# Block inverse of the second recurrence: transposes by VectorE on 32 by 32 blocks in place of TensorE

## The reference

```python
def wkv_scan(r, v, decay, k, a_in, b_in, s0, reverse):
    def step(S, inp):
        rt, vt, wt, kt, at, bt = inp
        sa = jnp.einsum('bhij,bhj->bhi', S, at)
        S = S * wt[:, :, None, :] + sa[..., None] * bt[:, :, None, :] + vt[..., None] * kt[:, :, None, :]
        return S, jnp.einsum('bhij,bhj->bhi', S, rt)
    xs = tuple(jnp.moveaxis(z, 1, 0) for z in (r, v, decay, k, a_in, b_in))
    s_end, ys = lax.scan(step, s0, xs, reverse=reverse)
    return jnp.moveaxis(ys, 0, 1), s_end
```

## Time and profile before

| | |
|---|---|
| median of three runs | 3336.87 us |
| the profiled execution, its own time | 3332.58 us |
| its span, first to last instruction | 3330.8 us |
| PE (TensorE matmul) busy | 3237.4 us, 97% of the span |
| PEld (TensorE weight load) busy | 2940.8 us, 88% |
| DVE (VectorE) busy | 2141.8 us, 64% |
| ACT (ScalarE) busy | 1547.5 us, 46% |
| mean granted TensorE clock | 0.992 of full speed |
| the 16 batches of the recurrence | about 2395 to 3150 us from the span's start |

### The profile page before, as it was taken

How to read it: one execution, slowest core, us unless ns; L and a number is a source line. 1 busy time by engine, 2 the same in 40 slices (tenths; PEclk the granted TensorE clock), 3 DMA queues, 4 the chain that set the end, 5 groups by cost and what they waited for, 6 DMA issues and landing times.

```text
span 3330.8 us, 82761 instructions
## 1 busy us (share of the span) xinstructions
PE 3237.4 (97%) x37068; PEld 2940.8 (88%) x37068; DVE 2141.8 (64%) x3294; ACT 1547.5 (46%) x2366; POOL 177.1 (5%) x254
## 2 busy tenths in 40 slices
PE   7999999999899999999999999999999999999988
PEld 7989999899788888888889888988889999999987
DVE  7655755667668888885555544445666766657565
ACT  5433443445444444444434444433555555556433
POOL 0000000000000000000001010001211101111010
PEclk9999999999999999999999999999999999999999
DMA  5645655765455555555553343435443344434464
GB/s 202 237 165 176 210 209 188 286 252 198 143 176 189 191 190 190 189 191 203 187 188 125 119 148 123 152 122 171 159 137 129 121 143 130 144 126 135 132 231 152
DMA packets 99713, 571.20 MB, mean 171 GB/s; under 512 B 19856, under 2 KB 26288, under 8 KB 37408
## 3 DMA queue, kind: packets, MB, share of 16 engines
q1 hardware_dynamic: 85872, 511.85, 44.5%
q0 software_dynamic: 13488, 54.06, 4.8%
HBM read 535.59 MB, written 30.28 MB: 170 GB/s over the span
## 4 chain that ended last, share of the span: by engine, by line
PE 85%; DVE 7%; issue 3%; ACT 3%; DMA 1%; POOL 0%; DVEq 0%; SPq 0%; ACTq 0%; POOLq 0%
PE banks L300 15%; PE banks L301 8%; PE banks L1069 4%; PE banks L2209 4%; PE banks L1070 4%; PE banks L1071 4%; PE banks L324 3%; PE banks L325 3%; PE banks L326 3%; PE banks L2210 3%; PE banks L2211 3%; PE banks L2431 3%; PE banks L287 3%; PE banks L288 3%; PE banks L289 3%
## 5 line engine op out<-in xcount | busy, mean ns | idle before, releaser
L267 DVE TENSOR_TENSOR w_lo<-ring,w_hi 128x2048 fp32r<-128x2048 f32 x274 | 629.5, 2298 | 420.8 <-ACT w_hi L261 420.8
L261 ACT CAST w_hi<-ring 128x2048 fp32r<-128x2048 f32 x274 | 522.7, 1908 | 228.8 <-PE banks L301 97.2
L300 PE MATMUL banks<-x_two,w_hi 128*128 128x512 f32 x1408 | 488.3, 394 | 0.0
L301 PE MATMUL banks<-x_two,w_lo 128*128 128x256 f32 x1408 | 390.0, 277 | 0.0
L1069 PE MATMUL banks<-x_two,w_hi 128*128 128x256 f32 x1152 | 344.2, 299 | 4.7 <-DVE w_lo L1143 2.4
L1070 PE MATMUL banks<-x_two,w_hi 128*128 128x256 f32 x1152 | 327.6, 284 | 0.0
L1071 PE MATMUL banks<-x_two,w_lo 128*128 128x256 f32 x1152 | 327.4, 284 | 0.0
L300 PEld LDWEIGHTS banks<-x_two,w_hi 128*128 128x128 f32 x1408 | 264.0, 188 | 61.4
L2209 PE MATMUL banks<-XK,w_hi 128*128 128x256 f32 x1024 | 304.1, 297 | 2.5 <-DVE w_lo L2265 2.4
L2210 PE MATMUL banks<-XK,w_hi 128*128 128x256 f32 x1024 | 289.5, 283 | 0.0
L2211 PE MATMUL banks<-XK,w_lo 128*128 128x256 f32 x1024 | 289.1, 282 | 0.0
(11 more groups left out here) (573 smaller groups left out, 7669.2 us busy)
## 6 DMA issues: line engine op xcount, KB each, us to landing
ring<-in_w_up SPq DMA_DIRECT2D x88, 1024.0 KB, 4.8
ring<-in_w_dil SPq DMA_DIRECT2D x72, 1024.0 KB, 5.1
mod_ring<-in_w_mod SPq DMA_DIRECT2D x48, 1024.0 KB, 6.9
ring<-in_w_logit SPq DMA_DIRECT2D x48, 1024.0 KB, 5.1
ring<-in_w_down SPq DMA_DIRECT2D x44, 1024.0 KB, 4.8
ring<-in_w_delta SPq DMA_DIRECT2D x32, 1024.0 KB, 4.9
ring<-in_w_out SPq DMA_DIRECT2D x32, 1024.0 KB, 4.8
ring<-in_w_na SPq DMA_DIRECT2D x32, 1024.0 KB, 4.9
```

The costliest lines, as they stand in the source:

```text
L261: nc.scalar.copy(w_hi[:, s, 0:w], ring[:, s, 0:w]).then_inc(S("panel_hi"), 4)
L267: nc.vector.tensor_tensor(w_lo[:, s, 0:w], ring[:, s, 0:w], w_hi[:, s, 0:w].bitcast(F32), ALU.subtract).then_inc(S("panel_split"), 4)
L300: nc.tensor.matmul(out_ap, hi, both, start=first_, stop=False)
L301: return nc.tensor.matmul(out_ap[:, 0, :], lo, both[:, 0, :], start=False, stop=last_)
```

## The change

TensorE's second product in s1 and in each `level_a` goes. In s1 ScalarE copies only the square to `iB`, and VectorE transposes `iB` to `iC` in 32 by 32 blocks (mark "c2"), which is the whole transpose as the square is zero outside its 8 by 8 diagonal blocks. In each level VectorE transposes `iX`'s blocks 4 to 7 to `iS` and blocks 0 to 3 to `iB` (mark "xt") ahead of the mask; `iX` is at that point zero outside diagonal blocks of 8, 16 or 32. ScalarE exchanges the halves: two copies of 64 by 256 from `iS` to `iB`, which wait for "xt" and no longer for "y".

```diff
-        dve_order += [("a", b), ("x0", b), ("aak", b)] * inv + [("bonus_in", it_)] * bonus
+        dve_order += [("a", b), ("x0", b), ("aak", b)] * inv + [("bonus_in", it_)] * bonus + [("c2", b)] * inv
...
         def level_a(b, l):
             pe.wait_ge(S("rw_dve"), vv("xl", b, l - 1) if l else vv("x3", b))
-            crossed(4, 0, iN, lambda q, m: iX[rows(q), m, :])
-            crossed(4, T, iX, lambda q, m: CT(7)[rows(q), :]).then_inc(S("rw_mm"), 1)
+            crossed(4, 0, iN, lambda q, m: iX[rows(q), m, :]).then_inc(S("rw_mm"), 1)
...
                 pe.wait_ge(S("rw_dve"), vv("a", b))
-                crossed(4, 0, iT, lambda q, m: iA[rows(q), m, :])
-                crossed(4, T, iA, lambda q, m: iT[rows(q), m, :]).then_inc(S("rw_mm"), 1)
+                crossed(4, 0, iT, lambda q, m: iA[rows(q), m, :]).then_inc(S("rw_mm"), 1)
...
                 pe.wait_ge(S("rw_act"), aa("b2", b))
-                pe.wait_ge(S("rw_dve"), vv("x0", b))
+                pe.wait_ge(S("rw_dve"), vv("c2", b))
...
         def turned(b, l):
-            act.wait_ge(S("rw_dve"), vv("y", b, l))
-            nc.scalar.copy(iBC[:, 0], pair(4, T, T)).then_inc(S("rw_act"), 1)
+            act.wait_ge(S("rw_dve"), vv("xt", b, l))
+            nc.scalar.copy(iB[0:CHUNK, 4:8, :], iS[CHUNK:P, :, :])
+            nc.scalar.copy(iB[CHUNK:P, 4:8, :], iS[0:CHUNK, :, :]).then_inc(S("rw_act"), 1)
...
-                nc.scalar.copy(iBC[:, :, :, :].rearrange("p k h c -> p h k c"),
-                               PS[:, 4:6, :].rearrange("p h (k c) -> p h k c", k=2)).then_inc(S("rw_act"), 1)
+                nc.scalar.copy(iBC[:, 0], pair(4, 0, T)).then_inc(S("rw_act"), 1)
...
         def masked(b, l):
+            dve.wait_ge(S("rw_dve"), vv("xl", b, l - 1) if l else vv("x3", b))
+            nc.vector.transpose(iS[:, :, :], iX[:, 4:8, :])
+            nc.vector.transpose(iB[:, 0:4, :], iX[:, 0:4, :]).then_inc(S("rw_dve"), 1)
+            vv.here("xt", b, l)
             dve.wait_ge(S("rw_mm"), mm("ya", b, l))
...
-            F(turns(i, "B"))
+            F(turns(i, "B") - 1)
+            if inv:
+                dve.wait_ge(S("rw_act"), aa("b2", b))
+                nc.vector.transpose(iBC[:, 1], iBC[:, 0]).then_inc(S("rw_dve"), 1)
+                vv.here("c2", b)
+            F()
```

More of the change, by code:

```diff
@@ L2378, in program @@
         act_order += [("x", b, 2)] * inv + [("sq", it_ - 1)] * back
-        dve_order += [("a", b), ("x0", b), ("aak", b)] * inv + [("bonus_in", it_)] * bonus
+        dve_order += [("a", b), ("x0", b), ("aak", b)] * inv + [("bonus_in", it_)] * bonus + [("c2", b)] * inv
         dve_order += [("state", s_, 0)] * st + [("x2", b), ("a4", b), ("x3", b)] * inv
-        dve_order += [("epi", it_ - 1)] * back2 + [("y", b, 0)] * inv
+        dve_order += [("epi", it_ - 1)] * back2 + [("xt", b, 0), ("y", b, 0)] * inv
         dve_order += [("xl", b, 0)] * inv + [("cum", b + 1), ("t", b + 1)] * nx + [("state", s_, 1)] * first_
         dve_order += [("s0", it_)] * back + [("blo", it_ - 1)] * back2
-        dve_order += [("y", b, 1)] * inv + [("yacc", s_)] * late
+        dve_order += [("xt", b, 1), ("y", b, 1)] * inv + [("yacc", s_)] * late
         dve_order += [("xl", b, 1)] * inv + [("bonus", it_)] * bonus
-        dve_order += [("y", b, 2)] * inv + [("ar", b)] * (inv and tau >= 2) + [("cent", it_ - 1)] * back
+        dve_order += [("xt", b, 2), ("y", b, 2)] * inv + [("ar", b)] * (inv and tau >= 2) + [("cent", it_ - 1)] * back
         dve_order += [("tilde", b + 1)] * nx + [("xl", b, 2)] * inv + [("varx", it_ - 1)] * back
```

## The result

| | before | after |
|---|---|---|
| median of six runs | 3339.97 us | 3318.80 us |
| lowest to highest | 3332.74 to 3348.11 us | 3313.35 to 3329.92 us |
| the profiled execution | 3332.58 us | 3329.92 us |
| ratio after to before, 95% interval | | 0.9947 (0.9929 to 0.9965) |

A forecast was written before the change was run, and what follows sets the result against it. The prediction took TensorE to bound the recurrence: 29.4 us off its stream, less 2.4, 0.9, 1.2, 1.7 and 0.5 us of lateness, is 22.7 us, so 3336.9 us becomes 3314 us. The range was 3304 to 3331 us.

The forecast's parts named there:

- What bounds the stage: From batch 1 to the recurrence's end TensorE bounds, busy 711.6 of 725 us; removed work is gain unless another engine lags.
- The price of a group: Each removed TensorE group of 32 matmuls in the levels and s1 saves 0.46 us; 64 groups save 29.4 us.
- The price of a transpose: VectorE transposes at the plain pace: 421 ns for 256 columns, 680 ns for 512; 46 us in all.
- The double rate: If VectorE's transpose ran like the 284 ns SBUF copy of 256 columns, the net gain would be 24.5 us, not 22.7.
- The list of places with nothing to spare: Hand-overs where TensorE would wait: `w_lo` of slots I, A, F cost 2.4, 0.9, 1.2 us; "c2" behind reciprocals 1.7.
- the ring: ScalarE already waits 27 us for panels, which are now wanted 4% sooner; 0.5 us lost.
- The size of what comes too late: Losses of TensorE's saving at late hand-overs across the stage: 2.4, 0.9, 1.2, 1.7 and 0.5 us, 6.7 us forecast.
- thin cover: Rival: VectorE's margins are thinner and slips add up between slots; losses double, 16 us less, 3321 us; chance 0.15.
- ScalarE at nothing: ScalarE's changed copies add 0.24 us per batch, on an engine idling 69.1 us at that copy: cost nothing.
- The scan's pace: Rival: VectorE transposes 128 columns in 402 ns, the pair and "c2" take 1.4 us each; 15 us left, 3322 us; chance 0.10.
- the dear transpose: Rival: VectorE's transpose turns the sign, zero gain near 1.2 us per 256 columns, near 3400 us at reciprocal's pace; chance 0.10.
- does not do what it says: Rival: panels, not TensorE, pace the stage, so TensorE waits out its saving; 3337 us; chance 0.05.

The follow-up runs named there:

- The last run: The kernel with three moves, with the two transposes of each level replaced by a one-column copy: stretch without issue gaps 669.9 us, ratio to before 0.9914.
- the early pair: The kernel with three moves, with level 2's two transposes put right behind the sum of level 1, ahead of `b_tilde`: 3304.0 us, ratio to before 0.9898.
- the pairs left out: The changed kernel with the two transposes of each level replaced by a one-column copy: stretch without issue gaps 676.3 us, ratio to before 0.9906.
- more transposes: The changed kernel plus an unused 256-column transpose in each level and an unused 512-column one in s1: ratio to before 0.9990.
- three moves: The changed kernel with slot I's first turn earlier, one reciprocal behind the square's transpose, and the epilogue's blo after slot F's turns: 3306.7 us, ratio 0.9914.

## Why the prediction was right, and where it was off

- **What bounds the stage**: right. With the VectorE work in place in both, taking TensorE's groups away, and making it wait for the transposes instead, gives 700.2 - 684.1 = 16.1 us. With VectorE's cost mostly gone it gives 27.3 us.
- **The price of a group, 0.46 us by the pitch of the weight loads**: right within a tenth. The last run gives 27.3 us for 60 groups. In the five batches without a new wait (3, 4, 7, 8 and 11) the change takes off 1.7 us without gaps for four groups, 0.43 us each, on the mean of the two profiles of each kernel. By that, 26 us came in the stretch, where 27.6 were forecast.
- **The price of a transpose**: right. I took 421 ns, or 375 with two back to back, for 256 columns, and 680 ns for 512 columns. The rows show 441 and 403 ns, and 710. The double rate of the one-source copy (284 ns) does not come. From 256 to 512 columns the time grows by some 0.29 us, 1.1 ns for each column, as it does for the other operations (421 to 690 ns). Section 3.8 of the Trainium skill's Vector Engine (DVE) Microarchitecture Reference has one element per cycle per lane for the transpose; the trace agrees so far as it shows one pace for the transpose and for these operations.
- **The list of places with nothing to spare**: right in the main. Of the 6.2 us by which the waits for `w_lo` grew, slot J of batches 1, 6, 10 and 14 has 2.3 (2.4 forecast, with batch 11, which does not wait), slot A of batches 6 and 14 has 1.3 (0.9) and slot G of batches 5, 9 and 13 has 1.2 (1.2). Slot J of batches 2, 5, 9 and 13, 1.4 us, was not on the list, and the 0.5 us for the ring shows in no wait. The transpose of the square in batch 5, VectorE and then TensorE:

```profile
2632.75 0.69 DVE L2265 TENSOR_TENSOR w_lo<-ring,w_hi 128x512 fp32r<-128x512 f32 x1
2633.36 0.70 DVE L3015 STREAM_TRANSPOSE iBC<-iBC 128x512 f32<-128x512 f32 x1
```

```profile
2634.21 0.27 PE L2431 MATMUL banks<-iX,iBC 64*64 64x64 f32 x2 [0.56 <-DVE iBC L3015]
```

The forecast was a wait of 0.7 us here, and it is 0.56. The three waits sum to 1.8 us against 1.7 forecast with batch 0 in it. That the sums agree is luck in part: the third is in batch 13, where I had seen room, and none is in batch 0.

- **The size of what comes too late**: this term was mis-sized. The forecast was 6.7 us; the stage shows about 12 (29.4 less the 17.1 gained, of which some 2 us are fewer issue gaps). TensorE's waits other than "issue" grew by 11.5 us: those for `w_lo` by 6.2 where the forecast had 5.0 in all, those for ScalarE's copies by 3.5 where it had nothing, and that of s2 by the 1.8 that it had. I had taken it that each idle time resets the slip. In batch 1 it does not. Before the change, level 2's mask and slot I's turns on VectorE:

```profile
2464.76 0.69 DVE L2958 TENSOR_TENSOR iA<-banks,consts 128x512 f32<-128x512 f32 x1 [0.92 <-PE banks L2431]
...
2468.51 1.28 DVE L2265 TENSOR_TENSOR w_lo<-ring,w_hi 128x512 fp32r<-128x512 f32 x2
```

and after it, VectorE, ScalarE and TensorE:

```profile
2470.11 0.69 DVE L2965 TENSOR_TENSOR iX<-banks,iX 128x512 f32<-128x512 f32 x1
2472.04 0.69 DVE L2860 TENSOR_TENSOR BT<-BT,LdE 128x512 f32<-128x512 f32 x1 [1.25 <-ACT Lc L2697]
...
2474.57 0.45 DVE L2956 STREAM_TRANSPOSE iS<-iX 128x256 f32<-128x256 f32 x1
2474.94 0.40 DVE L2957 STREAM_TRANSPOSE iBC<-iX 128x256 f32<-128x256 f32 x1
2475.27 0.65 DVE L2960 TENSOR_TENSOR iA<-banks,consts 128x512 f32<-128x512 f32 x1
...
2478.97 1.29 DVE L2265 TENSOR_TENSOR w_lo<-ring,w_hi 128x512 fp32r<-128x512 f32 x2
```

```profile
2466.97 0.41 ACT L2739 COPY iBC<-iS 64x256 f32<-64x256 f32 x1 [1.58 <-DVE iBC L2957]
...
2471.32 0.62 ACT L2697 ACTIVATE Lc<-Lc 128x512 f32<-128x512 f32 x1
```

```profile
2479.80 0.36 PE L2209 MATMUL banks<-XK,w_hi 128*128 128x256 f32 x1 [1.39 <-DVE w_lo L2265]
```

The sum of level 1 (L2965 at 2470.11) now has no idle time before it, since the pair of level 1 made VectorE late. Neither has the mask of level 2 (L2960 at 2475.27), which before had 0.92 us. TensorE's wait at slot J is 1.39 us, 0.84 more than the 0.55 before, where I had 0.28 more. The slip of level 1 is carried to level 2 behind `b_tilde` (L2860), and the 1.25 us of idle time before `b_tilde` do not reset it, as VectorE waits there for ScalarE's exponentials. ScalarE works without a break from its two copies, which wait for the pair of level 1, to the last exponential, so it is late by the same pair. From the start of the copies to that exponential it takes 4.35 us, where it took 3.99 with one copy (2456.63 to 2460.62 before the change). This is the mechanism of the rival "thin cover", slips that add up from slot to slot, and by size it came too: its 16 us against 17.1 measured in the stage, where the forecast was 22.7. Its share of the chances was 0.15, so the stage speaks more for this rival than for the forecast; that the forecast fits the whole times is in part their scatter. The idle time before the mask came out at 37 us where 25 was forecast; why is not shown.

- **Batch 0 was not costed.** I gave the spare time of `level_b` for batches 1 to 15 only. In batch 0, level 2, VectorE waits for ScalarE's exponentials and makes the pair behind them, ScalarE copies after that, and TensorE stands. VectorE, ScalarE and TensorE:

```profile
2431.04 0.69 DVE L2860 TENSOR_TENSOR BT<-BT,LdE 128x512 f32<-128x512 f32 x1 [2.22 <-ACT Lc L2697]
...
2432.97 0.45 DVE L2956 STREAM_TRANSPOSE iS<-iX 128x256 f32<-128x256 f32 x1
2433.34 0.40 DVE L2957 STREAM_TRANSPOSE iBC<-iX 128x256 f32<-128x256 f32 x1
```

```profile
2433.78 0.40 ACT L2739 COPY iBC<-iS 64x256 f32<-64x256 f32 x1 [1.42 <-DVE iBC L2957]
2434.19 0.40 ACT L2740 COPY iBC<-iS 64x256 f32<-64x256 f32 x1
```

```profile
2434.65 0.69 PE L2431 MATMUL banks<-iA,iBC 64*64 64x64 f32 x32 [1.78 <-ACT iBC L2740]
```

With 0.62 us at level 0 that is 2.4 us, which the forecast did not have. "x" no longer waits for the mask, but here it waits for a transpose that stands late in VectorE's order. In the run with the early pair 0.94 us of the 1.78 are left, as a wait for the mask.

- **ScalarE at nothing**: not right. Its own added work is small, but it hands VectorE's lateness on: to `level_b` in batch 0, to `solved` in batch 6 (L2729, 1.1 us, and 1.4 in the second profile), and to `b_tilde` in batch 1, where its two copies add 0.36 us of their own. With the pairs left out, 1.6 of the 2.4 us at `level_b` stay.
- **The rivals.** The scan's pace, the dear transpose and "does not do what it says" are excluded by the durations and by the stretch. But their slope was too flat: the sum for the dear transpose had the gain gone near 1.2 us for 256 columns, 2.9 times the price, and the run with more transposes has most of it gone at about 1.6 times, a part of that by the clock.

## What to carry to other kernels

Work moved to an idle engine is paid twice where a hand-over has nothing to spare: by its own length, and by what the first engine now comes sooner. The transposes cost 3 us beside the old stream, with nobody waiting for them; beside the shortened one and waited for, the pairs alone cost 7 us. After such a move, list each hand-over with its spare time and set the next order by it: three moves of a turn, a reciprocal and a subtraction took back 9 us of the 12 to 14 us lost in the stretch. A slip is reset only by an idle time longer than the slip, and not by one that waits for a third engine which the same slip has made late; so follow it through to the next slot instead of costing each place by itself. And before two profiles are compared within 2 us, count the times that TensorE's clock stood at half in each.

## What was not expected of the hardware

TensorE's gaps that nothing in the profile explains go with the program. In both profiles of the changed kernel they came in the same batches, but for two of 0.3 us. They are 5 to 11 us in the stretch, and between versions they moved by up to 4 us in one batch: batch 12 has none before, 1.7 us after and 4.2 us with three moves. What makes them was not tried. They also bear on the clock: five of the eight times at half clock began behind such a gap, the other three behind a wait.

Ahead of the recurrence, where both programs are the same, the changed kernel's profiled executions were slower twice. The mask of batch 0 starts at 2409.0 and 2408.4 us, and in all other kernels, those with further moves too, between 2393 and 2397.5. The time lies in the wide matmuls of the projections. Line 300 of the changed kernel, up to 2400 us, and then of the kernel before in its second profile:

```profile
L300 PE MATMUL banks<-x_two,w_hi 128*128 128x512 f32 x1408 | 497.7, 399 | 0.0
```

```profile
L300 PE MATMUL banks<-x_two,w_hi 128*128 128x512 f32 x1408 | 488.3, 394 | 0.0
```

399 ns against 394, over 1408 of them and as many of line 301, make 13 us, at a mean granted clock over the whole execution of 0.990 and 0.993. Its other runs, with medians of 3318.8 and 3317.3 us, show the whole gain of the stage, so most of them cannot have lost these 13 us. Why the profiled executions do is open.
